# The key/value block of a two-layer trunk on one core: how its slabs, its input and two small fetches are ordered

## The reference, cut to what matters

```python
def rms_norm(x, g):
    y = x * lax.rsqrt(jnp.mean(x * x, axis=-1, keepdims=True) + NORM_EPS)
    return y * g
...
for i in range(DEPTH):                       # 2
    a = rms_norm(h, g[0])
    if i % 2 == 0:                           # qkv = a @ w_qkv: 2048 q, 256 k, 256 v columns
        a = sliding_window_sink_attention(a, positions, w_qkv, w_o, sinks)
    else:
        a = sgu_mixer(a, w_in, ln_g, ln_b, w_s, b_s, w_out)
    h = h + rms_norm(a, g[1])
    c = jnp.square(jax.nn.relu(rms_norm(h, g[2]) @ w_up)) @ w_down
    h = h + rms_norm(c, g[3])
```

## Time and profile before

| what | value |
|---|---|
| time, median of 3 runs | 1971.51 us (1971.41 to 1972.63) |
| the profiled execution, span | 1971.5 us |
| TensorE busy | 1949.2 us, 99% |
| TensorE weight loads busy | 1604.2 us, 81% |
| VectorE busy | 1076.2 us, 55% |
| ScalarE busy | 972.2 us, 49% |
| mean granted clock of TensorE | 0.997 of full speed |
| read from main memory | 365.51 MB |

### The profile page before, as it was taken

One profiled execution on the slowest core, in us unless ns is written; L12 is line 12 of the kernel. 1 busy time (PEld: TensorE's weight loads), 2 busy tenths in 40 slices (PEclk: granted clock), 3 DMA queues, 4 the chain that ended last, 5 costly groups with the idle time before them and its releaser, 6 DMA issues.

```text
span 1971.5 us, 26643 instructions
## 1 busy us (share of the span) xinstructions
PE 1949.2 (99%) x8914; PEld 1604.2 (81%) x8914; DVE 1076.2 (55%) x1276; ACT 972.2 (49%) x1339; POOL 6.2 (0%) x23
## 2 busy tenths in 40 slices
PE   7999999999999999999999999999999999999998
PEld 5777888888888888888888888888888888888886
DVE  5666575454454455455667655654544554544455
ACT  6666465435434543454564445654355435434542
POOL 0000000000000000000000000000000000000000
PEclk9999999999999999999999999999999999999999
DMA  6634656555555555555475555565555555555553
GB/s 205 203 128 164 207 197 203 191 192 182 191 195 180 189 192 192 192 172 196 150 259 171 192 189 177 173 212 199 194 177 188 196 191 190 178 199 189 182 192 107
DMA packets 189833, 368.40 MB, mean 187 GB/s; under 512 B 12616, under 2 KB 12752, under 8 KB 189008
## 3 DMA queue, kind: packets, MB, share of 16 engines
q1 hardware_dynamic: 187264, 360.75, 54.8%
q0 software_dynamic: 1040, 6.82, 0.9%
q10 hardware_dynamic: 1472, 0.08, 0.0%
HBM read 365.51 MB, written 2.10 MB: 186 GB/s over the span
## 4 chain that ended last, share of the span: by engine, by line
PE 98%; DMA 1%; ACT 0%; DVE 0%; SPq 0%; issue 0%; DVEq 0%; ACTq 0%
PE acc L357 31%; PE acc L359 31%; PE acc L358 31%; PE t L378 2%; DMA w_raw<-in_attn_w_qkv 1%; PE t L391 1%; PE scores L459 0%; PE o L481 0%; PE t L469 0%; PE scores L591 0%; PE t L439 0%; ACT a_hi L650 0%; DVE w_lo L977 0%; DVE h L1014 0%; ACT w_hi L630 0%
## 5 line engine op out<-in xcount | busy, mean ns | idle before, releaser
L977 DVE TENSOR_TENSOR w_lo<-w_raw,w_hi 128x1024 fp32r<-128x1024 f32 x680 | 820.6, 1224 | 632.1 <-ACT w_hi L630 603.5
L630 ACT ACTIVATE w_hi<-w_raw 128x1024 fp32r<-128x1024 f32 x680 | 708.4, 1058 | 626.0 <-PE acc L359 590.9
L357 PE MATMUL acc<-w_hi,a_hi 128*128 128x512 f32 x1440 | 573.5, 398 | 4.8 <-DVE w_lo L977 4.4
L359 PE MATMUL acc<-w_hi,a_lo 128*128 128x512 f32 x1440 | 563.2, 391 | 0.0
L358 PE MATMUL acc<-w_lo,a_hi 128*128 128x512 f32 x1440 | 562.5, 391 | 0.0
L357 PE MATMUL acc<-w_hi,b_hi 128*128 128x512 f32 x1280 | 500.9, 391 | 0.0
L359 PE MATMUL acc<-w_hi,b_lo 128*128 128x512 f32 x1280 | 498.4, 389 | 0.0
L358 PE MATMUL acc<-w_lo,b_hi 128*128 128x512 f32 x1280 | 498.1, 389 | 0.0
L357 PEld LDWEIGHTS acc<-w_hi,a_hi 128*128 128x128 f32 x1440 | 271.3, 188 | 62.2 <-issue 7.5
L359 PEld LDWEIGHTS acc<-w_hi,a_lo 128*128 128x128 f32 x1440 | 271.2, 188 | 58.3
L358 PEld LDWEIGHTS acc<-w_lo,a_hi 128*128 128x128 f32 x1440 | 271.6, 189 | 53.5
(11 more groups left out here) (120 smaller groups left out, 475.6 us busy)
## 6 DMA issues: line engine op xcount, KB each, us to landing
w_raw<-in_mlp_w_up SPq DMA_DIRECT2D x256, 512.0 KB, 4.2
w_raw<-in_mlp_w_down SPq DMA_DIRECT2D x256, 512.0 KB, 4.4
w_raw<-in_sgu_w_in SPq DMA_DIRECT2D x64, 512.0 KB, 4.6
w_raw<-in_attn_w_qkv SPq DMA_DIRECT2D x40, 512.0 KB, 4.6
w_raw<-in_attn_w_o SPq DMA_DIRECT2D x32, 512.0 KB, 4.2
w_raw<-in_sgu_w_out SPq DMA_DIRECT2D x32, 512.0 KB, 4.4
gain<-in_norm_gains POOLq DMA_DIRECT2D x4, 1024.0 KB, 5.4
h<-in_x SPq DMA_DIRECT2D x8, 256.0 KB, 11.4
```

What stands on the lines that cost most here:

```text
L357: nc.tensor.matmul(acc[t][:, :], lhsT=x_hi[:, kb, tok], rhs=w1, start=(kb == 0), stop=False)
L359: last = nc.tensor.matmul(acc[t][:, :], lhsT=x_lo[:, kb, tok], rhs=w1, start=False, stop=(kb == KB - 1))
L630: nc.scalar.activation(w_hi[:, i % SLOTS, :], w_raw[:, i % RAW_SLOTS, :], ACT.Copy).then_inc(hi_made, 1)
L977: nc.vector.tensor_tensor(w_lo[:, i % SLOTS, :], w_raw[:, i % RAW_SLOTS, :], w_hi[:, i % SLOTS, :].bitcast(F32), ALU.subtract).then_inc(lo ...
```

## The change

- SP fetches x and slabs by turns (x0, slab 0, x1, slab 1, ... x7, slab 7) without a wait. For slabs 4 to 7 there are four more slots, `kv_raw`, which lie in y, not in use yet; they have semaphores of their own. The slots of w_raw are then filled with Q0's slabs 0 to 3, each once w_lo of the slab before in its slot is made; from Q0's slab 4 on all is as before.
- The units come by feature group: both tiles of group 0, both of group 1, and so on (X_UNIT). TensorE, in `kv_block`, takes slabs 0 and 1 of tile 0, then of tile 1, then slabs 2 and 3 of both, and so on. Units 2p + 2 and 2p + 3 are transposed after the second slab of tile 0 and after the first slab of tile 1 of pair p.
- ScalarE and VectorE split a unit and a slab by turns. The squares come after units 3, 4, 6 and 7. Both tiles are read out one after the other, after four slabs of Q0 are split (two before).
- The block accumulates in the scores' two banks, not in acc0 and acc1, and Q0's first products don't wait for its read-out. The gains pass through bank o0.
- Positions and sinks are fetched from ScalarE's queue after the last square, ahead of Q0's first slabs. The negated sinks are made on VectorE after Q0's rotation, not behind the angles.

The diff, cut to its core (removed lines of the old `first_block` and pure renames are left out):

```diff
+X_UNIT = [(pair, t) for pair in range(NB) for t in range(TOK)]
...
+        kv_raw = yf[:, :].rearrange("p (i n) -> p i n", i=RAW_SLOTS)
...
+        kv_landed = [sem(f"kv_landed{i}") for i in range(RAW_SLOTS)]
...
+        def raw(blk, i):
+
+            if isinstance(blk, int) and blk == B_KV and i >= RAW_SLOTS:
+                return kv_raw[:, i - RAW_SLOTS, :]
+            return w_raw[:, i % RAW_SLOTS, :]
+
...
-                pair, t = UNIT[n]
+                pair, t = X_UNIT[n]
...
-            for units, slabs in (([0], (0, 2)), ([1], (2, 3)), ([2, 3], (3, 4)), ([4], (4, 6)), ([5, 6, 7], (6, 8))):
-                for n in units:
-                    load_x(n)
-                load_block(B_KV, w_qkv[0], D, slabs=range(*slabs))
-            with sp.Fori(0, NB) as j:
+            def kv_source(i):
+                rows = w_qkv[0].rearrange("(k p) n -> p k n", p=P)
+                return rows[:, i * SLAB_KB:(i + 1) * SLAB_KB, D:D + COL]
+
+            for i in range(2 * PAIRS):
+                load_x(i)
+                sp.dma_start(raw(B_KV, i).rearrange("p (k n) -> p k n", k=SLAB_KB), kv_source(i)
+                             ).then_inc(slab_landed[i] if i < RAW_SLOTS else kv_landed[i - RAW_SLOTS], 16)
+            for i in range(RAW_SLOTS):
+                sp.wait_ge(lo_made, i + 1)
+                src = w_qkv[0].rearrange("(k p) n -> p k n", p=P)[:, i * SLAB_KB:(i + 1) * SLAB_KB, 0:COL]
+                sp.dma_start(w_raw[:, i, :].rearrange("p (k n) -> p k n", k=SLAB_KB), src).then_inc(slab_landed[i], 16)
+            load_block(B_Q, w_qkv[0], 0, slabs=range(RAW_SLOTS, 2 * PAIRS))
+            with sp.Fori(1, NB) as j:
                 load_block(j + B_Q, w_qkv[0], j * COL)
...
-            def multiply_slab(blk, x_hi, x_lo, i, t):
-
-
-                if i == 0:
-
-                    at_least(pe, acc_free, blk * 2 + (t - 1))
+            def multiply_slab(blk, x_hi, x_lo, i, t, bank=acc):
+
+
+                if i == 0 and not (isinstance(blk, int) and blk <= B_Q):
+
+                    pe.wait_ge(acc_free, blk * 2 + (t - 1))
...
+                    nc.tensor.matmul(bank[t][:, :], lhsT=x_hi[:, kb, tok], rhs=w1, start=(kb == 0), stop=False)
+                    nc.tensor.matmul(bank[t][:, :], lhsT=x_hi[:, kb, tok], rhs=w2, start=False, stop=False)
+                    last = nc.tensor.matmul(bank[t][:, :], lhsT=x_lo[:, kb, tok], rhs=w1,
...
-                pair, t = UNIT[n]
+                pair, t = X_UNIT[n] if first_layer else UNIT[n]
...
-            def first_block(blk, use0, first_layer=False):
+            def kv_block():
+
+                transpose_unit(0, 0, True)
+                transpose_unit(1, 0, True)
+                for pair in range(PAIRS):
+                    for t in range(TOK):
+                        for i in (2 * pair, 2 * pair + 1):
+                            pe.wait_ge(t_lo, X_UNIT.index((pair, t)) * 4 + (i % 2 + 1) * SLAB_KB)
+                            multiply_slab(B_KV, a_hi, a_lo, i, t, sc)
+                            if pair < PAIRS - 1 and (t, i % 2) in ((0, 1), (1, 0)):
+                                transpose_unit(2 * pair + 2 + t, 0, True)
+
+            def first_block(blk, use0):
 
 
                 order = [(t, i) for t in range(TOK) for i in range(6)] + [(t, i) for t in range(TOK) for i in (6, 7)]
 
                 units = {0: 2, 2: 3, 4: 4, 6: 5, 8: 6, 10: 7}
-                if first_layer:
-                    transpose_unit(0, use0, True)
...
+            nc.tensor.transpose(ob[0][:, 0:P], gain_rows[:, :], ident[:, :]).then_inc(small_filled, 1)
+
+
+            kv_block()
...
+                if not isinstance(blk, int) or blk > B_KV:
+
+                    act.wait_ge(slab_landed[i % RAW_SLOTS],
+                                blk * (32 * PAIRS // RAW_SLOTS) + 16 * (i // RAW_SLOTS))
+                elif i < RAW_SLOTS:
+                    act.wait_ge(slab_landed[i], 16)
+                else:
+                    act.wait_ge(kv_landed[i - RAW_SLOTS], 16)
...
+                nc.scalar.activation(w_hi[:, i % SLOTS, :], raw(blk, i), ACT.Copy).then_inc(hi_made, 1)
...
+            def load_positions():
+                act.dma_start(pos_i[:, :], positions[0].rearrange("(t p) -> p t", p=P),
+                              allow_slow_non_contiguous=True).then_inc(pos_landed, 16)
+
+            def load_sinks():
+                for i in range(2):
+                    act.dma_start(sink_rows[i * CHUNK:(i + 1) * CHUNK, :, :],
+                                  sinks[0].rearrange("(a i e) -> i a e", i=2, e=2)[i].partition_broadcast(CHUNK),
+                                  allow_slow_non_contiguous=True).then_inc(sinks_landed, 16)
...
+            def kv_block(evac):
+
+                squares = {3: (0, 0), 4: (1, 0), 6: (0, 1), 7: (1, 1)}
+                for i in range(2 * PAIRS):
+                    split_unit(i, 0, 0, X_UNIT)
+                    split_slab(B_KV, i)
+                    if i in squares:
+                        t, part = squares[i]
+                        for pair in (2 * part, 2 * part + 1):
+                            act.wait_ge(x_landed[X_UNIT.index((pair, t))], 16)
+                        square_h(t, part)
+                load_positions()
+                load_sinks()
+                split_next(B_KV, 2, 3, 4)
+                take_root()
+                split_next(B_KV, 5)
+                act.wait_ge(norm_done, norms[0])
+                evac(0)
+                evac(1)
+                split_next(B_KV, 6, 7)
+
...
-            act.dma_start(pos_i[:, :], positions[0].rearrange("(t p) -> p t", p=P),
-                          allow_slow_non_contiguous=True).then_inc(pos_landed, 16)
-            for i in range(2):
-                act.dma_start(sink_rows[i * CHUNK:(i + 1) * CHUNK, :, :],
-                              sinks[0].rearrange("(a i e) -> i a e", i=2, e=2)[i].partition_broadcast(CHUNK),
-                              allow_slow_non_contiguous=True).then_inc(sinks_landed, 16)
...
-            nc.scalar.activation(gain_cols[:, :], sc[0][:, 0:P], ACT.Copy).then_inc(small_copied, 1)
+            nc.scalar.activation(gain_cols[:, :], ob[0][:, 0:P], ACT.Copy).then_inc(small_copied, 1)
...
+                once = sc[t][:, 0:256].rearrange("p (g d) -> p g d", g=KVH)
...
-                nc.scalar.activation(v_band[:, 2 * t, :], acc[t][:, 256:512], ACT.Copy, scale=r_in[:, t:t + 1]
+                nc.scalar.activation(v_band[:, 2 * t, :], sc[t][:, 256:512], ACT.Copy, scale=r_in[:, t:t + 1]
...
+                nc.vector.tensor_tensor(w_lo[:, i % SLOTS, :], raw(blk, i),
...
+            def input_norm():
...
                 sums[0] += 2 * TOK
                 dve.wait_ge(norm_sum, sums[0])
                 link(nc.vector.tensor_tensor(sum_sq[:, :], pre_ssq[:, 0, :], pre_ssq[:, 1, :], ALU.add))
                 mean()
                 inverse(r_in)
...
+            def kv_block():
+
+                for i in range(2 * PAIRS):
+                    split_unit(i, 0, 0, X_UNIT)
+                    split_slab(B_KV, i)
+                split_next(B_KV, 2, 3)
+                input_norm()
+                split_next(B_KV, 4, 5)
+                rotary_angles()
+                split_next(B_KV, 6, 7)
...
-                dve.wait_ge(sinks_landed, 32)
-                link(nc.vector.tensor_scalar(neg_sink[:, :, :, :], sink_rows[:, :, :].rearrange("p (g a) e -> p g e a", a=2),
-                                             -1.0, None, ALU.mult))
...
+            dve.wait_ge(sinks_landed, 32)
+            link(nc.vector.tensor_scalar(neg_sink[:, :, :, :], sink_rows[:, :, :].rearrange("p (g a) e -> p g e a", a=2),
+                                         -1.0, None, ALU.mult))
```

More of the change, by code:

```diff
@@ L642, in split_ahead, with split_unit @@
                 split_next(blk, 2 * pair, 2 * pair + 1)
-            def split_unit(n, use0, norm):
-                pair, t = UNIT[n]
+            def split_unit(n, use0, norm, order=UNIT):
+                pair, t = order[n]
                 act.wait_ge(t_filled, use0 + n + 1)
@@ L675, in first_block @@
+            def first_block(blk, use0, norm, evac):
                 h0 = h_seen[0]
-                h_seen[0] += 0 if layer0 else UNITS
+                h_seen[0] += UNITS
                 def square(t, part):
-                    if layer0:
-                        for pair in (2 * part, 2 * part + 1):
-                            act.wait_ge(x_landed[UNIT.index((pair, t))], 16)
-                    else:
-                        act.wait_ge(h_ready, h0 + UNIT.index((2 * part + 1, t)) + 1)
-                    square_h(t, part)
@@ L711, in first_block @@
                 square(1, 1)
-                if not layer0:
-                    split_next(blk, 3)
+                split_next(blk, 3)
                 take_root()
@@ L976, in split_slab @@
                 dve.wait_ge(hi_made, blk * (2 * PAIRS) + (i + 1))
-                nc.vector.tensor_tensor(w_lo[:, i % SLOTS, :], w_raw[:, i % RAW_SLOTS, :],
```

(25 more changed lines are left out.)

73 lines of the change are left out of this document (9 added, 64 removed).

## The result

| | before | after |
|---|---|---|
| time, median of 9 runs each | 1971.66 us (1971.32 to 1972.63) | 1976.88 us (1974.85 to 1977.69) |
| span of the profiled execution | 1971.5 us | 1975.7 us |
| TensorE busy | 1949.2 us | 1950.7 us |

The ratio of the times is 1.0022, interval 1.0014 to 1.003. The changed kernel is slower: by 5.2 us between the medians, 4.2 us between the spans, where 2.5 us less was predicted. TensorE is busy 1.5 us longer, with the same 8914 matrix instructions recorded.

A forecast was written before the change was run, and what follows sets the result against it. Took TensorE, busy 99% of the span, as the bound; only removing its stops could pay. 3.5 us won in the key/value block less 0.9 waiting for keys gave 2.6; 1971.5 - 2.5 = 1969.0 us, range 1966.5 to 1973.2.

The forecast's parts named there:

- case A: Whole kernel, main forecast: block 3.5 us earlier, 0.9 stop for keys; 1969.0, own range 1967.4 to 1970.6, chance 0.50.
- case C: Rival, Q0: slabs 4 and 5 land after 9 and 10 us, stop over 4, clock falls; 1974.7 to 1977, chance 0.07.
- Part 1, loads: Key/value block: at 0.33 MB/us x and slabs land before they are wanted, slab 3 at 12; DMA leaves the path.
- Part 2, first product: Start of key/value block: TensorE's first product starts at 9.1, 2.1 us earlier.
- Part 3, coupling: Key/value block: new order couples three engines, 8.6 us per period with paired stops; block ends at 41.7, 3.5 us earlier.
- Case F: Rival, key/value block: no coupling, ScalarE finds its inputs early, block ends at 36.2; gain 9, 1962.5, chance 0.10.
- Part 4, issue cost: ScalarE after the last square: the three moved fetches put 0.85 us of issue on the path, ends 0 and 1.9.
- the wait of 0.9 for the keys: Q0: keys' transposes fall due at 50.1 but start at 51.0, so TensorE stops about 0.9 us.
- Part 4, slabs 4 and 5: Q0: these two loads have 4.7 us each where such a load takes 4.6; no price, no reserve.
- B: Rival, Q0: small packets still in flight, slabs 4 and 5 land after 6.1 and 7.4 us; 1971.1, chance 0.16.
- D, the clock in short stops: Rival, key/value block: clock does not hold in stops of 1.5 us, block ends 3.8 later; 1971.9, chance 0.08.
- The base: Sum for the whole kernel: took the profiled execution's 1971.5 as the median's 1971.5 and subtracted 2.5 us.

The follow-up runs named there:

- rows_early: Changed kernel with sinks fetched as 128 rows of 128 bytes and both units of the next pair transposed after tile 0's first slab: 1965.35 us, ratio 0.9962.
- sinks_rows: Changed kernel with the sinks fetched at the same place in one fetch of 128 rows of 128 bytes, negated in two operations: 1970.09 us, ratio 0.9991.
- early_t: Changed kernel, small packets kept, with both units of the next pair transposed after the first slab of tile 0: 1970.85 us, ratio 0.9989.
- sinks_pool: Changed kernel with the sinks' same small fetches issued by GpSimd's queue at 36.0 instead of ScalarE's: 1979.41 us, ratio 1.0034.

## Why the prediction was wrong

The forecast was case A, 1969.0 us, range to 1973.2. What happened is case C, which had 0.07 and 1974.7 to 1977: stop over 4 us (4.86), clock down, transposes at 56.8 (56.21), 1976.88 us. C had the mechanism, but its time was met with some luck: each of its terms was too large (3.5 won where 2.2 was, 6.7 of stop where 5.03 was, 2.4 of clock where 1.41 was), and they partly cancel.

- **Part 1, loads: right.** In 8 to 12 us SP's queue moved 839 packets and 1.59 MB, against 384 and 0.73; ScalarE waited for no landing from 6 to 45 us.
- **Part 2, first product: 10.04, not 9.1.** The gains came later, transposed at 4.97 instead of 4.16, and all that hangs on them with it. In the three traces with the old order this lies between 3.89 and 4.30, in the seven with the new one between 4.33 and 4.97: part of these 0.8 us is scatter, and part seems to come with the new order of fetches; why was not tried. The first product, at 9.39 to 10.04 in all seven, never came at 9.1.
- **Part 3, coupling: right, and the best part.** Stops of 0.39, 0.55, then 0.39 and 1.40 in pairs, where 0.55, 0.65, then 0.4 and 1.5 were named. From first product to Q0 it took 32.98, predicted 32.6. Its end, 43.02 instead of 41.7, is the late start and 0.4. Case F (no coupling) falls for this kernel; its 36.2 for the end of an uncoupled block is close to what rows_early reached, 36.70. The period was put at 8.6 and measured 8.69 (first transposes at 22.93 and 31.62), though the terms listed for it add up to only 8.5. What I did not draw from it: 6 us of ScalarE's and TensorE's idling could be had back by moving one line.
- **Part 4, issue cost: 0, the lower end.** I took 0.85. The issues at 34.21, 34.64 and 35.38 lie under a running square and the unit after it, 3 us before the last square, behind which they stand in the program, had even started (37.21). And the wait of 0.9 for the keys that the sum took off does not exist without the packets: in sinks_rows the rotation ends at 50.72 and the transposes come at 51.10 without a stop.
- **Part 4, slabs 4 and 5: the step that failed.** "4.7 each, where such a load takes 4.6. No price, no reserve." The price of 4.6 is the median of forty loads, nearly all of them far from any small packet, and it was applied where the sinks' packets are in flight. The two loads took 10.2 and 10.3; that made the stop of 4.86 us and the slow products behind it, where the sum had 0.9 and none. In sinks_rows, without the small packets, they took 3.7 and 4.0.
- **The rivals' evidence.** Against B and C stood that the large queue is empty until 40, and against C that no load is queued ahead. Both are true and prove nothing: the small packets are not held up by large ones. In 36 to 40 us they moved 420 with nothing beside them, in 8 to 12 us before 391 beside 384 large ones. At the latter rate, which the prediction held in its hand, 1024 packets from 34.6 last to 45.1, and by its own walk the loads of slabs 4 and 5 are issued at 40.4 and 41.5, while they are still coming. B and C together deserved more than A.
- **B against C.** By turns, packet for packet, the loads would have got half and landed after 6.1 and 7.4. The Trainium skill, "DMA: Bandwidth & Descriptors", section "Queues, rings and completion order", states that each DMA engine goes round the queues that have work, packet by packet, and that such a packet can hold many descriptors. The stretch of before looks like turns of one (391 to 384); 386 to 0 in 40 to 44 us and 172 to 35 in 44 to 46 us do not, and turns piece by piece are refuted there. Whether the rule itself fails is open, since no run here shows how many of the profile's packets make one turn.
- **D, the clock in short stops: refuted.** The stops of 1.40 us left it at full level. The 4.86 us stop did not, and its 1.41 us is less than the 2.4 I had for C, since it rose again within 59 to 60 us. That price is not a constant: in early_t the clock stayed low until 55 us, and the two transposes lie 55.14 - 49.19 = 5.95 apart instead of 3.2, 2.7 more.
- **The base.** I set the profiled execution's 1971.5 equal to the median's 1971.5. The first is a span; in every later kernel the time is 1.7 to 1.9 us above the span. The profiled execution was thus probably at 1973.3, above all nine times of the table, and a forecast made against it should have been put 1.8 above its own span. It did not decide the result, and it accounts for the medians differing by 5.2 and the spans by 4.2. (The sum also turned its own 2.6 into 2.5.)

**Still open.** What makes the sinks' packets slow, and what holds the large queue at zero. Each sink packet is in the record with little time of its own (4.3% of 16 engines for 386 packets in 4 us is 7 ns each), and yet an engine takes one only every 150 ns (16 engines, 106 per us). Smallness alone isn't it, since the positions' packets went at 356 per us (178 in 0.5 us). The sinks' fetch reads the same few numbers for every partition and scatters eight pieces into each; sinks_rows also reads the same numbers for all, but in one piece each, and is fast. Which of count of pieces per partition, shape or alignment makes the pace was not tried. In sinks_pool the recorded packets fill the engines, in the others they don't, and the record does not say which of the two forms tells how long an engine is held. Nor does a run here tell why the loads got their turn at the start and not at 40 us.

## What to carry to other kernels

Look at a fetch's packets and its time to land, not at its bytes: here 8 KB in 1024 pieces were in flight for 14 us and more than doubled the landing time of loads issued meanwhile, and 16 KB in 128 rows landed in 2.9 us, with loads behind it landing in 4.0. Before such a fetch is moved, write down which loads are issued in the stretch where it will be in flight, price them as the loads that stood beside it before, and follow the delay to everything that the waiting engine still owes; if the form of the fetch can be changed, try that first: here it beat both places, in both orders. In a hand-written order ask for each unit of work whether the engine that makes it ready could have had it one step earlier.

## What the hardware showed that I had not expected

- The sinks' packets are slow by themselves: about 100 per us whether beside loads (391 in 4 us), alone (420 in 4 us), or from another issuing queue (10.5 us to land, as from ScalarE's). The Trainium skill, "DMA: Bandwidth & Descriptors", section "Issuing engines are not separate DMA queues", says that fetches of all engines run on the same 16 DMA engines; sinks_pool agrees, with 12.2 us for a load that takes 3.7 in sinks_rows.
- A queue of loads can get nothing at all beside them: 0 packets against 386 in 40 to 44 us.
- Fetches that stand behind a square, a unit, a slab and another square in ScalarE's program were issued from the start of the first of these on (34.21 to 36.02 us), and the operations kept their pace: 1.00 us from the unit to the slab, 0.95 from the slab to the square.
- Stops of 1.40 and 1.80 us of TensorE did not lower the clock (1.00 in 30 to 31 us of the kernel after); stops of 2.57, 3.60, 3.68, 4.40, 4.86 and 6.82 us were followed by slow products at 0.50.
